# Two-layer decoder trunk: the token mixers' projections in another order, with their own loads, two copies on ScalarE, and one FFN remainder in halves

## What is computed

```python
h = rmsnorm(x, ln_attn[l])
proj = h @ w_in                      # q, 6 k/v groups, gates, conv_in (512), retention q, k, v, gate (256 each)
o_a = nsa_mixer(...)                 # 8 heads: compressed, selected and window attention, gated
o_b = conformer_conv(conv_in, ...)   # a * sigmoid(g), depthwise causal convolution of 31 taps, layer norm, silu, @ conv_pw
o_c = retention(rq, rk, rv, rg, ..)  # 4 heads: rotary, decayed scores, group norm, silu gate
x = x + concat([o_a, o_b, o_c]) @ w_out
h = rmsnorm(x, ln_ffn[l])
x = x + (swiglu(h, ...) if l % 2 == 0 else moe_ffn(h, ...))   # dense, then 8 experts, top 2
```

## Time and profile before

| | us |
|---|---|
| three timed executions | 1283.48, 1283.83, 1285.69 (median 1283.83) |
| the profiled execution | 1281.99 |
| its span in the trace | 1280.0 |
| TensorE busy | 1255.0 (98%) |
| VectorE busy | 999.7 (78%) |
| ScalarE busy | 853.0 (67%) |

### The profile page before, as it was taken

The page is one execution under the profiler, slowest core; times in us unless marked ns, Lnnn a source line. Parts: engine busy times, 40 slices in busy tenths (PEclk is TensorE's granted clock), DMA queues, the critical chain, the costliest instruction groups (busy, mean ns, idle before and its releaser), DMA issues.

```text
span 1280.0 us, 16275 instructions
## 1 busy us (share of the span) xinstructions
PE 1255.0 (98%) x6319; PEld 1016.4 (79%) x6319; DVE 999.7 (78%) x1114; ACT 853.0 (67%) x1219; POOL 31.2 (2%) x21
## 2 busy tenths in 40 slices
PE   9999999999999899999999999999999999999997
PEld 7887578888789776788888888888888888888885
DVE  3698455545448955998899889999889889889897
ACT  3525364444443454878888888878878878878885
POOL 0000000000000000010000000000000000000300
PEclk9999999999999999999999999999999999999999
DMA  9333194552521335899999999999999999999981
GB/s 391 141 143 131 38 372 182 198 197 102 197 99 71 142 132 212 344 401 381 382 371 377 391 373 369 391 381 370 387 377 376 387 371 365 388 375 356 417 365 44
DMA packets 35649, 367.62 MB, mean 287 GB/s; under 512 B 4080, under 2 KB 4208, under 8 KB 8048
## 3 DMA queue, kind: packets, MB, share of 16 engines
q1 hardware_dynamic: 32832, 356.56, 70.6%
q0 software_dynamic: 1440, 5.24, 1.1%
q10 hardware_dynamic: 1296, 4.72, 0.9%
HBM read 360.73 MB, written 5.77 MB: 286 GB/s over the span
## 4 chain that ended last, share of the span: by engine, by line
PE 91%; DVE 6%; ACT 2%; issue 1%; DMA 0%; DVEq 0%; SPq 0%; ACTq 0%
PE ps L650 87%; PE ps L653 4%; DVE arena L1594 1%; DVE wlU L1828 1%; DVE blocks L1649 1%; DMA x<-x_in 0%; DVE arena L1667 0%; DVE wlD L1835 0%; DVE arena L1740 0%; ACT arena L1277 0%; ACT xn L1185 0%; ACT L1259 0%; ACT L1314 0%; DVE xn L2070 0%; ACT whU L1359 0%
## 5 line engine op out<-in xcount | busy, mean ns | idle before, releaser
L1828 DVE TENSOR_TENSOR wlU<-ring,whU 128x2048 fp32r<-128x2048 f32 x198 | 453.4, 2290 | 64.1 <-ACT whU L1359 59.4
L1359 ACT ACTIVATE whU<-ring 128x1024 fp32r<-128x1024 f32 x396 | 417.7, 1061 | 60.7 <-PE ps L650 53.1
L650 PE MATMUL ps<-whU,hTh 128*128 128x512 f32 x880 | 352.9, 401 | 1.7 <-DVE wlU L1828 1.7
L650 PE MATMUL ps<-whU,hTl 128*128 128x512 f32 x880 | 345.0, 392 | 0.0
L650 PE MATMUL ps<-wlU,hTh 128*128 128x512 f32 x880 | 343.0, 390 | 0.0
L1835 DVE TENSOR_TENSOR wlD<-ring,whD 128x2048 fp32r<-128x2048 f32 x97 | 222.1, 2290 | 39.2 <-ACT whD L1371 39.1
L1371 ACT ACTIVATE whD<-ring 128x1024 fp32r<-128x1024 f32 x194 | 205.3, 1067 | 58.9 <-PE ps L650 52.6
L650 PEld LDWEIGHTS ps<-whU,hTl 128*128 128x128 f32 x880 | 165.2, 188 | 36.1
L650 PEld LDWEIGHTS ps<-whU,hTh 128*128 128x128 f32 x880 | 165.3, 188 | 33.8 <-DVE wlU L1828 2.5
L650 PEld LDWEIGHTS ps<-wlU,hTh 128*128 128x128 f32 x880 | 166.1, 189 | 32.4
L650 PE MATMUL ps<-whD,gTh 128*128 128x512 f32 x428 | 168.7, 394 | 0.4 <-DVE gTl L1853 0.4
(11 more groups left out here) (231 smaller groups left out, 1233.3 us busy)
## 6 DMA issues: line engine op xcount, KB each, us to landing
ring<-moe_in SPq DMA_DIRECT2D x88, 2048.0 KB, 8.6
ring<-moe_in SPq DMA_DIRECT2D x88, 1024.0 KB, 8.9
ring<-ffn_in SPq DMA_DIRECT2D x11, 2048.0 KB, 7.6
ring<-mix_in SPq DMA_DIRECT2D x6, 3072.0 KB, 11.7
ring<-ffn_in SPq DMA_DIRECT2D x11, 1024.0 KB, 7.1
ring<-mix_in SPq DMA_DIRECT2D x4, 2048.0 KB, 10.3
ring<-mix_in SPq DMA_DIRECT2D x2, 2176.0 KB, 8.1
ring<-mix_in SPq DMA_DIRECT2D x2, 2112.0 KB, 8.1
```

The costliest lines, as they stand in the source:

```text
L650: return nc.tensor.matmul(o, lhsT, rhs, start=first, stop=last, skip_group_check=True)
L1359: A(whU[:, p, :], ring[:, f.slot(J), p * PIECE:(p + 1) * PIECE], ACT.Copy).then_inc(s_hi, 1)
L1828: V.tensor_tensor(wlU[:, w, :], raw, whU[:, w, :].bitcast(F32), ALU.subtract).then_inc(s_lo, 1)
```

## The change

In both openings the convolution's `cg` and `ca` come ahead of retention's `rvg`, and the taps are spread anew: six parts in `OPEN` instead of two, seven in `HEAD`, three beside the units instead of six. `reto` and `convT` move from unit 3 to unit 2, `hid` 0 from unit 2 to unit 3, `cnorm` 0 to unit 3, `retnorm` 0 to unit 4 ahead of `cnorm` 1. In layer zero the columns of `cg` and `ca` have loads of their own with semaphores of their own, ahead of `RET`; the second token tile is loaded ahead of the parameters. The copies of `ks` and `reto` go from VectorE to ScalarE. Layer one's piece 0 is split at the end of `dense`. `lo_up` makes its first remainder of step 1 in two subtractions. The places of `whM` are assigned by a table, and 14 warming products stand where 20 stood.

```diff
-BESIDE = {0: [("rets", 0)] + conv(10, 12), 1: [("rets", 1)] + conv(12, 14), 2: [("hid", 0)] + conv(14, 16),
-          3: [("reto", 0), ("convT", 0)], 4: [("cnorm", 0), ("croot", 0), ("hid", 1)],
-          5: [("cnorm", 1), ("retnorm", 0)],
+BESIDE = {0: [("rets", 0)] + conv(13, 15), 1: [("rets", 1)] + conv(15, 16), 2: [("reto", 0), ("convT", 0)],
+          3: [("hid", 0), ("cnorm", 0)], 4: [("croot", 0), ("hid", 1), ("retnorm", 0)], 5: [("cnorm", 1)],
...
-EARLIER = (("stat", 0), ("nT", 0), ("stat", 1))
+EARLIER = (("stat", 0), ("nT", 0), ("stat", 1), ("piece", 0))
...
+HOME = (0, 1, 2, 3, 1, 2, 0, 3)
+HELD = {4: ("cg", 0), 5: ("ca", 0), 7: ("rqk", 1)}
...
+            def conv_columns(a, b):
+                src = mix_in[0, MIX_OFF[LOADS[CONV][0]]:MIX_OFF[LOADS[CONV][0] + 1]].rearrange("(p k n) -> p k n", p=P, k=KD)
+                dst = item(0, CONV)[:, 0:KD * 768].rearrange("p (k n) -> p k n", k=KD)
+                return sp.dma_start(dst[:, :, a:b], src[:, :, a:b])
...
+                elif n == CONV:
+                    conv_columns(0, FC).then_inc(slot_full[n % SLOTS], 16)
...
-            sp.dma_start(par[:], params_in).then_inc(s_par, 16)
             sp.dma_start(x[:, 1, :], x_in[P:2 * P, :]).then_inc(s_x[1], 16)
+            sp.dma_start(par[:], params_in).then_inc(s_par, 16)
...
+                    if l == 0 and m == RET:
+                        conv_columns(2 * FC, 3 * FC).then_inc(s_conv_in[0], 16)
+                        conv_columns(FC, 2 * FC).then_inc(s_conv_in[1], 16)
...
-                        keep_busy(ps[:, 0, :], 20)
+                        keep_busy(ps[:, 0, :], 14)
...
+                    elif stage == "ks":
+                        full(act, l, stage)
+                        for g in range(2):
+                            z = slice(g * HD, (g + 1) * HD)
+                            last = A(kT[z, g, :, :], bank(l, stage)[z, :].rearrange("p (c t) -> p c t", c=2), ACT.Copy)
+                        is_free(last, l, stage)
+                    elif stage == "reto":
+                        full(act, l, stage)
+                        is_free(A(ro[:].rearrange("p i h d -> p (i h d)"), bank(l, stage), ACT.Copy), l, stage)
...
                 turned(DENSE, STEPS - 1)
+                piece(1, 0)
...
+                if J == 1 and h == 0:
+                    for p in range(2):
+                        dve.wait_ge(s_hi, f.up(J, p) + 1)
+                        last = V.tensor_tensor(wlU[:, p, :], ring[:, f.slot(J), p * PIECE:(p + 1) * PIECE],
+                                               whU[:, p, :].bitcast(F32), ALU.subtract)
+                    last.then_inc(s_lo, 1)
+                    return
```

More of the change, by code:

```diff
@@ new lines @@
+        [("stat", 0), ("nT", 0), ("stat", 1), ("piece", 0), ("split", 0), ("vsw", 0), ("nT", 1), ("piece", 1), ("rqk", 0),
+         ("split", 1), ("vsw", 1), ("piece", 2), ("piece", 3), ("rqk", 1), ("cg", 0), ("ca", 0)] + conv(0, 1) + [("piece", 4),
+         ("piece", 5)] + conv(1, 3) + [("rvg", 0), ("piece", 6)] + conv(3, 6) + [("rvg", 1)])
+HEAD = [("rqk_end", 0)] + conv(6, 7) + [("rqk_end", 1)] + conv(7, 8) + [("piece", 7), ("q", 0), ("retT", 0)] + conv(8, 10) + \
+       [("q", 1), ("retT", 1)] + conv(10, 12) + [("ks", 0)] + conv(12, 13) + [("kcv", 0), ("score", 0), ("score", 1), ("kcv", 1)]
@@ L398, in hybrid_trunk_kernel @@
         home_at = (arena_at + 4 * 6144, arena_at + 4 * mix_at["catT"], arena_at + 4 * mix_at["rp0"], xn_at)
-        whM = [nc.alloc_sbuf_tensor_at(f"whM{h}", [P, KD, FC], F32R, offset=home_at[h]) for h in range(HOMES)]
+        whM = [nc.alloc_sbuf_tensor_at(f"whM{h}", [P, KD, FC], F32R, offset=home_at[h]) for h in range(4)]
         beforeb = sb("beforeb", [P, P], BF16)
@@ L478, in hybrid_trunk_kernel @@
         s_rk = sem("s_rk")
+        s_conv_in = [sem(f"s_conv_in{h}") for h in range(2)]
         s_gather = sem("s_gather")
@@ L677, in width_major @@
                 for k in range(KD):
-                    last = three(o, whM[n % HOMES][:, k, w], low[:, k, w], hTh[:, k, :], hTl[:, k, :], k == 0, k == KD - 1)
+                    last = three(o, whM[HOME[n]][:, k, w], low[:, k, w], hTh[:, k, :], hTl[:, k, :], k == 0, k == KD - 1)
                 return last
@@ L685, in split_major @@
                 for k in range(KD):
-                    last = three(o, hTh[:, k, t], hTl[:, k, t], whM[n % HOMES][:, k, :], low[:, k, :], k == 0, k == KD - 1)
+                    last = three(o, hTh[:, k, t], hTl[:, k, t], whM[HOME[n]][:, k, :], low[:, k, :], k == 0, k == KD - 1)
                 return last
@@ L1201, in inverse_root, with piece @@
                 return A(o, var, ACT.Exp, scale=-0.5)
+            def piece(l, k):
+                m = SPLITS[k][0]
+                n = mix_load(l, m)
+                if l == 0 and k in (CG, CA):
+                    act.wait_ge(s_conv_in[k == CA], 16)
+                else:
+                    act.wait_ge(slot_full[n % SLOTS], filled(n))
+                if l == 0 and m == VW:
+                    act.wait_ge(s_half, 16)
+                if k == KS:
+                    act.wait_ge(s_rk, l + 1)
+                elif k in HELD:
+                    full(act, l, *HELD[k])
+                elif k == RQK_Q:
+                    full(act, l, "nT", NT - 1, 1)
+                A(whM[HOME[k]][:], piece_of(ring, l, k), ACT.Copy).then_inc(s_mhi, 1)
             def mixer(l):
@@ L1219, in mixer @@
                     elif stage == "piece":
[L1220 to L1231 removed]
+                        piece(l, k)
                     elif stage == "q":
@@ L1602, in conv_part, with piece @@
                             made[0] += 1
+            def piece(l, k):
+                dve.wait_ge(s_mhi, len(SPLITS) * l + k + 1)
+                V.tensor_tensor(piece_of(ringl, l, k), piece_of(ring, l, k), whM[HOME[k]][:].bitcast(F32),
+                                ALU.subtract).then_inc(s_mlo, 1)
             def mixer(l):
@@ L1626, in mixer @@
                     elif stage == "piece":
-                        dve.wait_ge(s_mhi, len(SPLITS) * l + k + 1)
-                        V.tensor_tensor(piece_of(ringl, l, k), piece_of(ring, l, k), whM[k % HOMES][:].bitcast(F32),
-                                        ALU.subtract).then_inc(s_mlo, 1)
-                    elif stage == "ks":
-                        full(dve, l, stage)
-                        for g in range(2):
-                            z = slice(g * HD, (g + 1) * HD)
-                            last = V.tensor_copy(kT[z, g, :, :],
-                                                 bank(l, stage)[z, :].rearrange("p (c t) -> p c t", c=2))
-                        is_free(last, l, stage)
+                        piece(l, k)
                     elif stage == "kcv":
```

36 lines of the change are left out of this document (7 added, 29 removed).

## The result

The changed kernel takes 1288.79 us (median of 20 runs, 1281.03 to 1290.11); the kernel before, run beside it, 1283.47 us (1281.60 to 1285.69). The ratio over all runs is 1.0034, with a 95% interval of 1.0024 to 1.0044. The forecast was 1281.4 us with a range up to 1284.4, and slower had a chance of 0.11. It was wrong by 7.4 us, and on the wrong side of "no change".

The account below looks back on a forecast made before the run. TensorE was taken to bound the openings, and VectorE's fixed order to be what TensorE mostly waits for in the middles. Terms -2.4 - 1.0 + 0.95 = -2.45 us on 1283.83 gave 1281.4 us, range 1278.6 to 1284.4.

Parts of the forecast that it names:

- the clock rival: In both layers' middle the new 2.2 us wait lowers the clock for 3 us: +3, 1284.4 us; chance 0.10.
- that row: Stretch 505 to 508 us after tiny products, clock at 0.50; taken as the length of a fall, 3 us.
- Middle, "Gain 1.2 us in each layer": Attention units after the projections: VectorE loses 4.9 us of taps per layer, ScalarE's copy comes sooner; 2.4 us in all.
- The transposes in unit 6: Middle: transposes of the normed convolution would wait about 0.9 us for the norm moved behind the other one.
- Halves, 1.0 us: First dense FFN step: remainder made in two halves, so TensorE's 0.83 us wait goes; gain 1.0 us.
- Seam, "Loss 0.95 us": Between the layers: layer one's first split delays the last dense sums and TensorE's transposes; loss 0.95 us.
- Opening, 0: Both layers' projections: products only reordered, TensorE sets the time, column loads land in time; 0.
- Experts, 0: Experts' first step: TensorE would come a microsecond sooner and wait a microsecond longer, about 1.4 us; 0.
- The sum: Whole kernel: -2.4 - 1.0 + 0.95 = -2.45 us, set on the median of 1283.83, giving 1281.4 us.
- the halfway point: Range's lower end, halfway to the rival where all middle waits go, 1274.2 us; chance 0.15 for better than 1279.5.

Follow-up runs that it names:

- decay-first kernel: Changed kernel with the last three groups of taps behind retention's second decay, convolution's transposes in unit 3, both norms one unit later: 1276.22 us, ratio 0.9940.

## Why the prediction was wrong

**The step that failed is the clock rival: "If the clock falls to its lower level (1.2 instead of 2.4 GHz) for as long as in that row, 3 us, the work in it takes 1.5 us longer ... Chance 0.10."** The mechanism was named, at the right instruction, with the right wait (2.2 forecast, 2.50 measured). Its chance and its size were wrong. 16 of the 20 executions have a time of 1288 us or more at a clock of 0.988 to 0.991; the three at 1283.5 to 1285.4 us (0.993 and 0.994) may have it in part, which no trace shows, as the kernel before comes to 0.994 too. In the trace it lasted 6.8 and 10 us, not 3, and cost 3.00 and 4.67 us in the two middles, against 1.5 each. That the middle had stood at 1.00 with 4.8 us of waits was read as evidence that it bears waits; but those waits are single ones of at most 1.22 us with work between them, and the sum over a stretch says nothing on one of 2.5. The one row with a fallen clock was used as if it gave the length of every fall, when no row bounded it from above.

At the routing the low stretch is 3.4 us in the trace of before and 6.8 in that of the changed kernel. In the other kernels without warm products there it takes 3.4 or 6.8 us, and what decides its length stays open. The Trainium skill, "TensorE: Matmul & The Clock Gate", Part 1, says of a kernel's start that the number of products which run at the lower clock differs between runs of the same kernel. For a fall in a kernel's midst there is one trace of each kernel here, so no run shows this directly, but the times spread as if it held there too: 1281.03 to 1290.11 us for the changed kernel, 1280.80 to 1289.98 with three warm products.

**Point by point:**
- *Middle, "Gain 1.2 us in each layer".* With the clock held by warm products it is 0.62 (30.03 less 29.41). The copy of unit 6's transposes on ScalarE comes at 109.57 us there, 110.1 in the old times (unit 1's values' product is 0.53 us earlier), where the forecast had 109.5: the term was mis-sized by 0.6 us. Some 0.36 us of it come first: retention's product starts 0.36 us behind the end of the decay's record (93.07 against 92.71 in the changed kernel), and the forecast let it start at once. The transposes in unit 6 wait for the norm as forecast, 0.53 us (0.78 with the clock held) where it had 0.9. In the old order the same twelve fewer taps gave 1.18 us, and with the decays first 3.24.
- *Halves, 1.0 us.* 1.09 in the changed kernel, 1.11 by the run without them. Right.
- *Seam, "Loss 0.95 us".* 0.91 in the trace, 0.87 by the run without it. But "What it buys is a free VectorE at 354 us, where TensorE is bound and it buys nothing" is wrong: in the new opening of layer one it takes away a wait of 2.14 us and a fall of the clock, 3.05 us in all on the decay-first kernel. The opening was not only reordered, it reads the piece earlier.
- *Opening, 0.* Right: TensorE is busy in the whole stretch from 12 to 82 us, its last projection record starts at 81.41 us in place of 81.44, and ScalarE takes the second and third piece at 16.48 and 20.05 us without a wait for their loads. From 12 to 17 us, with 1698 of 1708 packets under 2 KB, the DMA moved 360 GB/s, above the upper bound of 330 that was put for such loads.
- *Experts, 0.* Right in sum, wrong in its place: the waits of 0.83 us for the remainder (at 518.74) and of 0.43 us are now 0.79 us, ahead of the remainder's second half, and 0.46 us, not one of 1.4.
- *The sum.* With the terms as measured and the clock held it would be -1.24 - 1.09 + 0.91 = -1.4 us; the run with 9 products took 1281.5 us where before took 1284.5 beside it. The arithmetic on waits stands within a microsecond or two; the time was decided by the speed at which the work between them ran. (The range's lower end, 1278.6, is not the halfway point of 1277.8 that its words give; nothing hangs on it.)

Shown by runs: that the wait and its fill decide (one order, VectorE's work the same, 0, 3, 9 or 18 products), that exchanging the two products does it in the old kernel, that the middle keeps its clock with all other parts of the change in place. Open: why layer one's fall is longer than layer zero's. The length of the wait alone doesn't say it: behind 2.50 us in both layers the falls are 6.8 and 10 us, behind 3.93 us in both they are 6.8 and 3.4.

## What to carry to other kernels

When a change merges two short waits of TensorE into a long one, price the clock and not only the wait: here 2.50 us of unbroken idle time in place of 1.22 cost 7.7 us over the two layers. Read the clock column for every stretch, since work at half the clock shows as busy. Before an instruction is moved forward, look at what it waits for and move that with it; where that can't be done, products that depend on nothing can fill it: here nine (1.16 us of the 2.5) held the clock and cost nothing, and three (0.50 us) did not hold it. A part that looks like a loss alone (the split at the seam) is to be tried within the new order and not only priced against the old.

## What the runs showed that I had not expected

- One program can fall into several times by the clock alone: with idle times of 0.73 and 1.26 us around three short products, one of 12 runs kept 0.997 and nine had 0.989 to 0.991; with 0.73 and 0.61 us none of 11 left 0.995 to 0.999. Before, 0.73 and 1.22 us with 1.93 us of work between them kept 1.00 in its trace; but two of its 53 executions beside the experiments took 1287.2 and 1287.5 us at a clock of 0.992, so that kernel too has an execution with a lower clock now and then, and no trace shows where in it.
- The moment of the fall is not tied to one point of the wait: behind waits of the same 2.50 us it came 2.6 us after TensorE was at work again in layer zero, and already in the wait's last microsecond in layer one (0.78 in 433 to 434 us).
- Sixteen products of 256 columns between the router's 32 products of 8 columns cost only 0.5 us (3.98 against 3.49 us) and held the clock through the routing.
